# A Fourier mixing block in f32: the mix projection with its weights standing and the tokens moving, and two modulation vectors summed mostly on TensorE

## The chip, the cores and the metric

One core of a Trainium2 chip runs the whole kernel. The metric is the time of one execution on the device in microseconds (us); lower is better. Everything is f32 in memory. The large products are made of "f32r" parts: each operand is split into a high part and a low rest, and three one-pass products stand for one f32 product. The mix projection, the row sums and the transposes use plain f32 matmuls, which the trace shows as two records each (transposes as one).

## The reference, cut to what matters

512 tokens (N), 2048 channels (D), one layer of kind 0. The modulation vectors come from `c` by a 2048 x 12288 weight matrix, of which each vector takes 2048 columns.

```python
mod_x = silu(c) @ w_ada + b_ada
sh1, sc1, ga1, sh2, sc2, ga2 = split(mod_x, 6)
hx = rmsnorm(x, g_norm_mix) * (1 + sc1) + sh1
f  = fftn(hx.reshape(1, n, 4, 512), axes=(1, 3), norm='ortho').real
x  = x + ga1 * (f.reshape(1, n, 2048) @ fno_w_out)
h2 = rmsnorm(x, g_norm_ffn) * (1 + sc2) + sh2
x  = x + ga2 * (square(relu(h2 @ w_ffn_in)) @ w_ffn_out)
return rmsnorm(x, g_final)
```

## The kernel before, in words

Each engine has its own program, ordered by hand; semaphores join them. SP issues nearly all loads in one fixed order (`units`, with the mix tiles put between by `mix_after`). A load of 1 MiB goes into one of four slots (`raw`), and before load u SP waits until load u - 4 is consumed (`consumed`, line 369); whatever comes later in the list waits behind it. Mix tiles have four slots of their own (`load_mix`, line 395), freed by PE.

The stages, in order:

- To about 113 us: norm of x, the transform along the tokens, scale 1, the transform along the channels, and most of shift 1. The channel transform leaves cosine and sine parts for half of the tokens (`fe`, `fd`); the other half follows from symmetry, so that the projection has an even part and an odd part, whose sum and difference are the two token halves.
- Mix projection. 16 units (d, q): output columns 512d to 512d + 511, quarter q of the channels. A unit loads 1 MiB of `w_mix`; VectorE turns it into two combinations (`mix_sums`, lines 921 and 924). PE holds 128 tokens of `fe` or `fd` as weights and moves 512 columns of `w_mix`: four matmuls in `even_part` (line 1439), four in `odd_part` (1450) and two for a single middle row (`row_part`, 1460); with q = 3, three more for the first channel row. A bank holds 128 tokens x 512 channels, so the gate 1 vector has to be spread over all partitions (`row_sums`, line 1375). When a d is complete, ScalarE and VectorE combine, gate and add it to x (`combine`, `update_x`), and ScalarE squares it for the norm (line 577).
- Beside it the vectors gate 1, scale 2 and shift 2. A vector's load of 1 MiB is one weight row tile k (128 rows x 2048 columns; 8 KB to a partition), or two half rows of shift 2 (4 KB pieces); VectorE multiplies it by silu(c) and adds (`gemv`, line 823; `shift2_unit`, line 1020). The last five tiles of scale 2 go to PE (`gemv_rows`, line 1325): four matmuls with 32 equal weight columns, each in its own column group of the array, 512 columns moved by each.
- The turn to the FFN: last update, squares, root, `diag` (line 1072).
- First sweep (`up_step`, line 1561): 16 steps k. For each, PE turns 128 channels of x by matmuls with `diag` (`turn_tokens`, line 1534), ScalarE scales, shifts and makes the high part (lines 635 and 639), VectorE the low part (line 1085), and PE makes 12 products of 512 columns. The up weights are split by `up_high` and `up_low` (lines 607 and 1061). The second half of shift 2 is still added by VectorE in the sweep. At its end ScalarE takes the relu in two halves (line 656).
- The rest of the FFN: 15 periods of up and down products, then the final norm.

GpSimd writes x to HBM (line 462) for the end and loads the rows of gate 2 into `gate_w` (line 466).

## Time and profile before

| | |
|---|---|
| median of 3 runs | 1648.82 us (1647.47 to 1649.15) |
| span of the profiled execution | 1651.0 us; no other time of it is given |
| PE busy | 1606.8 us, 97% |
| VectorE busy | 1266.2 us, 77% |
| ScalarE busy | 545.4 us, 33% |
| moved by DMA | 272.64 MB, 165 GB/s over the span |

All times below count from the start of the span. "Busy" does not count waiting. Matmuls overlap each other in the trace, so what a matmul costs is read from one start to the next, not from its duration. `PEld` is the loading of weights, beside PE. A releaser ("<-") is what an idle engine waited for last.

### The profile page before, as it was taken

How to read it: one execution, taken by the hardware profiler on the slowest of the kernel's cores; microseconds unless marked ns; L12 is line 12 of the kernel's file. 1: busy time of each engine (PE TensorE's matmuls, PEld its weight loads, DVE VectorE, ACT ScalarE, POOL GpSimd, SP SyncE). 2: the span in 40 equal slices, each digit the busy share in tenths (PEclk: the TensorE clock that was granted, in tenths of full speed). 3: DMA queues.
4: the chain of work that ended last, by engine and by line, in shares of the span. 5: the costliest groups of instructions: out<-in, count | busy, mean ns of one | idle time of the engine just before them, and what ended most of it. 6: DMA issues, size and time to landing. Idle time of an engine off the chain costs nothing.

```text
span 1651.0 us, 18364 instructions
## 1 busy us (share of the span) xinstructions
PE 1606.8 (97%) x7009; PEld 1235.1 (75%) x7009; DVE 1266.2 (77%) x1168; ACT 545.4 (33%) x659; POOL 16.8 (1%) x30
## 2 busy tenths in 40 slices
PE   6989999999999999999999999999999999999997
PEld 5653332688888888888888888888888888888875
DVE  6758996748888888886868686868677777777878
ACT  5420002453333333333333333333333333333332
POOL 0000000100000000000000000000000000000000
PEclk9999999999999999999999999999999999999998
DMA  9999997924544444342323233323223323333352
GB/s 355 362 409 342 410 340 271 351 97 129 177 132 174 135 171 146 135 128 79 124 85 118 92 111 101 102 102 102 102 102 102 102 102 102 102 102 102 103 203 102
DMA packets 96970, 272.64 MB, mean 165 GB/s; under 512 B 4332, under 2 KB 5660, under 8 KB 85020
## 3 DMA queue, kind: packets, MB, share of 16 engines
q1 hardware_dynamic: 93664, 249.91, 42.3%
q0 software_dynamic: 3120, 22.07, 3.8%
q8 instruction: 30, 0.49, 0.1%
q14 instruction: 12, 0.10, 0.0%
q10 hardware_dynamic: 144, 0.07, 0.0%
HBM read 263.64 MB, written 8.39 MB: 165 GB/s over the span
## 4 chain that ended last, share of the span: by engine, by line
PE 87%; DVE 8%; DMA 3%; issue 2%; ACT 1%; SPq 0%; DVEq 0%; ACTq 0%
PE banks L1307 16%; PE banks L1308 16%; PE banks L1309 16%; PE banks L1613 11%; PE banks L1615 11%; PE banks L1617 11%; DMA raw<-in_w_ada 2%; DVE acc_s L823 1%; DVE acc_a L823 1%; DVE acc_b L1020 1%; PE banks L1534 1%; PE banks L1325 1%; DVE mixw L921 1%; DMA mixw<-in_w_mix 1%; PE banks L1450 1%
## 5 line engine op out<-in xcount | busy, mean ns | idle before, releaser
L1146 DVE TENSOR_TENSOR stp<-raw,stp 128x1024 fp32r<-128x1024 f32 x330 | 402.0, 1222 | 154.9 <-ACT stp L690 152.2
L690 ACT ACTIVATE stp<-raw 128x1024 fp32r<-128x1024 f32 x330 | 343.0, 1054 | 521.7 <-PE banks L1309 231.3
L1307 PE MATMUL banks<-acts,stp 128*128 128x512 f32 x1024 | 399.7, 390 | 0.0
L1308 PE MATMUL banks<-acts,stp 128*128 128x512 f32 x1024 | 398.4, 389 | 0.0
L1309 PE MATMUL banks<-acts,stp 128*128 128x512 f32 x1024 | 398.4, 389 | 0.0
L1613 PE MATMUL banks<-stp,hid 128*128 128x512 f32 x840 | 326.8, 389 | 0.0
L1615 PE MATMUL banks<-stp,hid 128*128 128x512 f32 x840 | 326.8, 389 | 0.0
L1617 PE MATMUL banks<-stp,hid 128*128 128x512 f32 x840 | 326.8, 389 | 0.0
L1167 DVE TENSOR_TENSOR dacc<-dacc,banks 128x1024 f32<-128x1024 f32 x202 | 245.5, 1215 | 14.2 <-PE banks L1617 14.2
L1309 PEld LDWEIGHTS banks<-acts,stp 128*128 128x128 f32 x1024 | 192.2, 188 | 40.0
L1307 PEld LDWEIGHTS banks<-acts,stp 128*128 128x128 f32 x1024 | 192.3, 188 | 39.8 <-DVE stp L1146 0.4
L1308 PEld LDWEIGHTS banks<-acts,stp 128*128 128x128 f32 x1024 | 192.2, 188 | 39.4
L1613 PEld LDWEIGHTS banks<-stp,hid 128*128 128x128 f32 x840 | 157.7, 188 | 32.9 <-DVE stp L1146 0.2
L1617 PEld LDWEIGHTS banks<-stp,hid 128*128 128x128 f32 x840 | 157.7, 188 | 32.7
L1615 PEld LDWEIGHTS banks<-stp,hid 128*128 128x128 f32 x840 | 157.7, 188 | 32.7
L668 ACT ACTIVATE hid<-hsum 128x512 fp32r<-128x512 f32 x45 | 28.5, 632 | 138.1 <-DVE hsum L1109 93.5
L823 DVE SCALAR_TENSOR_TENSOR acc_s<-raw,silu,acc_s 128x2048 f32<-128x2048 f32 x27 | 63.4, 2349 | 5.1 <-DMA raw<-in_w_ada 3.3
L1439 PE MATMUL banks<-mixw,fe 128*128 128x512 f32 x128 | 63.5, 619 | 1.8 <-DVE w_first L956 1.0
L1450 PE MATMUL banks<-mixw,fd 128*128 128x512 f32 x128 | 62.6, 614 | 0.0
L1122 DVE TENSOR_TENSOR raw<-raw 128x1024 f32<-128x1024 f32 x30 | 36.7, 1223 | 32.0 <-DMA raw<-in_w_ffn_out 32.0
L1097 DVE TENSOR_TENSOR sq<-sq 128x1024 f32<-128x1024 f32 x32 | 37.8, 1221 | 29.5 <-ACT sq L656 29.5
L668 ACT ACTIVATE hid<-sq 128x512 fp32r<-128x512 f32 x60 | 37.4, 624 | 68.5 <-DVE sq L1106 62.4
(190 smaller groups left out, 1227.1 us busy)
## 6 DMA issues: line engine op xcount, KB each, us to landing
raw<-in_w_ada SPq DMA_DIRECT2D x80, 1024.0 KB, 8.2
raw<-in_w_ffn_in SPq DMA_DIRECT2D x64, 1024.0 KB, 7.3
raw<-in_w_ffn_out SPq DMA_DIRECT2D x64, 1024.0 KB, 5.1
mixw<-in_w_mix SPq DMA_DIRECT2D x16, 1024.0 KB, 10.3
gate_w<-in_w_ada POOLq DMA_DIRECT2D x16, 1024.0 KB, 5.3
xres<-in_x SPq DMA_DIRECT2D x4, 1024.0 KB, 9.0
xmix_d<-xres POOLq DMA_DIRECT2D x4, 1024.0 KB, 12.7
xmix<-xmix_d SPq DMA_DIRECT2D x4, 1024.0 KB, 8.0
```

The costliest lines, as they stand in the source:

```text
L668: nc.scalar.activation(hid[:, a, :, 0, :], quarters[a], ACT.Copy).then_inc(h_hi, 1)
L690: nc.scalar.activation(stp[:, slot, 0, :, :], source.rearrange("p (a n) -> p a n", a=2), ACT.Copy).then_inc(w_hi, 1)
L823: ins = nc.vector.scalar_tensor_tensor(acc[:, :], source, silu[:, k:k + 1], acc[:, :], ALU.mult, ALU.add)
L1146: nc.vector.tensor_tensor(stp[:, slot, 1, :, :], source.rearrange("p (a n) -> p a n", a=2), stp[:, slot, 0, :, :].bitcast(F32), ALU.subtra ...
L1167: nc.vector.tensor_tensor(dst, dst, banks[:, b:b + 2, :], ALU.add).then_inc(d_read, 1)
L1307: nc.tensor.matmul(bank, w_hi_ap, m_hi, start=first, stop=False)
L1308: nc.tensor.matmul(bank, w_hi_ap, m_lo, start=False, stop=False)
L1309: return nc.tensor.matmul(bank, w_lo_ap, m_hi, start=False, stop=last)
L1450: mm = nc.tensor.matmul(banks[:, 4 * (d % 2) + 2 + tt, :], fd[:, 2 * q + i, tok], mixw[n % MIX_SLOTS][:, 2 + i, :], start=(q == 0 and i == 0),
L1613: nc.tensor.matmul(banks[:, b + tt, :], hid[:, q, kk, 0, tok], stp[:, slot, 0, kk, :], start=(kk == 0 and q not in (2, 3, 6)), stop=False, ...
L1615: nc.tensor.matmul(banks[:, b + tt, :], hid[:, q, kk, 0, tok], stp[:, slot, 1, kk, :], start=False, stop=False, skip_group_check=True)
L1617: mm = nc.tensor.matmul(banks[:, b + tt, :], hid[:, q, kk, 1, tok], stp[:, slot, 0, kk, :], start=False, stop=kk == HALF_T - 1, skip_group ...
```

## The change

The mix projection is turned around. Tile n (16 of them) is 128 output channels: PE holds 128 x 128 pieces of `w_mix` as weights and moves the frequencies: eight pieces and the first channel row over 257 columns (even part), eight over 255 (odd part), into one bank of 128 channels x 512 tokens. The host lays `w_mix` out so that a tile is 16 KB in a row for each partition, and gives a turned copy of x (`x_turned`, four loads of 1 MiB). Channels now lie on partitions: gate 1, scale 2 and shift 2 are single numbers of a partition. Gate 1 is summed by VectorE as before, then turned by PE. VectorE updates x (`xnew`), ScalarE squares it, VectorE adds the squares up, PE sums them over the partitions and spreads the inverse root (bank 4). PE turns each updated tile back (`turn_back`) to be written to HBM. Scale 2 and shift 2 come in eight blocks v of 512 columns (scale 2 for even v), each in four loads q of four row tiles (2 KB pieces): 32 loads, of which VectorE adds three ((0,0), (1,0), (2,0)) and PE 29; a load is 16 matmuls of 32 weight columns by 128 moved columns. Nine of PE's are in tiles 10 to 15, two between the mix and the sweep, 18 in the sweep. VectorE now scales in the sweep (`h2_scaled`) and ScalarE adds the shift. `turn_tokens`, `row_part`, `combine`, `update_pairs`, `shift2_unit` and the spread gate go. The cosine table is a third smaller.

Lines taken out in `up_step` stand with a minus; of the rest only what is new or kept around it is shown, and blank lines are left out.

```diff
+    BLOCKS = [(j, b) for b in range(DB) for j in (SCALE2, SHIFT2)]
+    ROWS_BY_DVE = [(0,)] * 3 + [()] * 5
+    rows_by_pe = lambda v: [q for q in range(UK) if q not in ROWS_BY_DVE[v]]
...
+    loads = [("raw", w) for w in units]
+    loads.insert(len(loads) - SHIFT_LAST, ("mix", 0))
+    loads.append(("mix", 1))
+    gates = [("ada", GATE1, k) for k in range(DT)]
+    blocks = [("block", v, q) for v in range(len(BLOCKS)) for q in range(UK)]
+    for n in range(2, 10):
+        loads += [("raw", w) for w in gates[2 * (n - 2):2 * (n - 1)]] + [("mix", n)]
+        if n >= 6:
+            loads.append(("turned", n - 6))
+    for n in range(10, MU):
+        loads += [("mix", n)] + [("raw", w) for w in blocks[2 * (n - 10):2 * (n - 9)]]
+    left = blocks[2 * (MU - 10):]
     up_units = [("up", q) for q in range(DT // UK)]
+    tail = up_units[0:2] + left[0:12] + up_units[2:3] + left[12:] + up_units[3:4]
+    loads += [("raw", w) for w in tail]
+    units = [w for kind, w in loads if kind == "raw"]
...
+    GATE1_AT = 8
+    UPDATED = {9: (0, 1), 10: (2, 3), 11: (4, 5, 6), 12: (7, 8, 9), 13: (10, 11), 14: (12, 13), 15: (14,)}
+    BLOCKS_AT = {10: [(0, 1)], 11: [(0, 2), (0, 3)], 12: [(1, 1)], 13: [(1, 2), (1, 3)], 14: [(2, 1)],
+                 15: [(2, 2), (2, 3)]}
+    BLOCK_BY_DVE_AT = {0: 10, 1: 12, 2: 14}
+    BLOCK_ROWS_AT = {0: 11, 1: 13, 2: 15}
+    TURN_BLOCK_AT = {0: 12, 1: 14}
+    BLOCK_TURNED_AT = {0: 12, 1: 14}
+    LATE_BLOCKS = {1: [(3, 2), (3, 3)], 2: [(4, 0), (4, 1)], 3: [(4, 2), (4, 3)], 4: [(5, 0), (5, 1)],
+                   5: [(5, 2), (5, 3)], 7: [(6, 0), (6, 1)], 8: [(6, 2), (6, 3)], 9: [(7, 0), (7, 1)],
+                   10: [(7, 2), (7, 3)]}
+    LATE_ROWS_AT = {3: 1, 4: 3, 5: 5, 6: 8, 7: 10}
+    LATE_TURN = {3: 3, 4: 5, 5: 6, 6: 10, 7: 11}
+    LATE_TURNED_AT = {2: 2, 3: 3, 4: 5, 5: 7, 6: 10, 7: 11}
+    UP_LATE_AT = {4: 5, 5: 6, 6: 10, 7: 12}
...
+            for kind, w in loads[1:]:
+                if kind == "mix":
+                    load_mix(w)
+                elif kind == "turned":
+                    load_turned(w)
+                else:
+                    u = position[w]
+                    if u >= RAW:
+                        sp.wait_ge(*consumed(units[u - RAW]))
+                    load(w, u % RAW)
...
+            def mix_copy(n):
+                act.wait_ge(w_used, n + 1)
+                nc.scalar.activation(xnew[:, n, :], banks[:, n % MIX_BANKS, :], ACT.Copy).then_inc(mix_out, 1)
+            def square(n):
+                act.wait_ge(updated, 2 * (n + 1))
+                if n >= 2:
+                    act.wait_ge(square_added, n - 2)
+                dst = square_sum if n == 0 else (square_even, square_odd)[n % 2]
+                nc.scalar.activation(dst[:, :], xnew[:, n, :], ACT.Square).then_inc(square_made, 1)
...
+            for n in range(MU):
+                turned_now = UPDATED.get(n - 1, ())
+                if n == MU - 1:
+                    up_high(0)
+                    up_high(1)
+                for u in turned_now[:1]:
+                    back_copy(u)
+                mix_copy(n)
+                for u in turned_now[1:]:
+                    back_copy(u)
+                for v in range(len(BLOCKS)):
+                    if BLOCK_ROWS_AT.get(v) == n:
+                        rows_of_block(v)
+                if n == GATE1_AT:
+                    rows_of(3)
+                for u in UPDATED.get(n, ()):
+                    square(u)
+            square(MU - 1)
+            back_copy(MU - 2)
             up_high(2)
             act.wait_ge(mean_done, 3)
             nc.scalar.activation(rms[:, 1, :], mean[:, 1, :], ACT.Sqrt).then_inc(rms_done, 1)
+            back_copy(MU - 1)
...
             for k in range(DT):
+                h2_high(k)
+                for m in range(4, UPS):
+                    if UP_LATE_AT[m] == k:
+                        up_high(m)
+                for v in range(len(BLOCKS)):
+                    if LATE_ROWS_AT.get(v) == k:
+                        rows_of_block(v)
...
+            def turned_block(v):
+                j, b = BLOCKS[v]
+                tiles = slice(GT * b, GT * (b + 1))
+                dve.wait_ge(rows_turned, 5 + v)
+                sums = banks[:, 7, P * (v % 4):P * (v % 4 + 1)].rearrange("p (a r) -> p a r", a=GT)[:, :, 0]
+                nc.vector.tensor_tensor(mods[:, j, tiles], sums, vec_t[:, j * DT + GT * b:j * DT + GT * (b + 1)],
+                                        ALU.add).then_inc(mod_step, 1)
+                if j == SCALE2:
+                    dve.wait_ge(mod_step, mods_after(v) - 1)
+                    nc.vector.scalar_tensor_tensor(mods[:, j, tiles], mods[:, j, tiles], 1.0,
+                                                   vec_t[:, 7 * DT + GT * b:7 * DT + GT * (b + 1)], ALU.add,
+                                                   ALU.mult).then_inc(mod_step, 1)
...
+            def update_x(n):
+                dve.wait_ge(mix_out, n + 1)
+                if n % GT == 0:
+                    dve.wait_ge(turned_in[n // GT], 16)
+                even, odd, new = xnew[:, n, 0:HALF], xnew[:, n, HALF:N], half_new[:, n % 2, :, :]
+                nc.vector.scalar_tensor_tensor(new, even.unsqueeze(1).to_broadcast([P, 2, HALF]),
+                                               mods[:, GATE1, n:n + 1],
+                                               xt[:, n, :].rearrange("p (a n) -> p a n", a=2),
+                                               ALU.mult, ALU.add).then_inc(update_half, 1)
+                dve.wait_ge(update_half, n + 1)
+                nc.vector.scalar_tensor_tensor(even, odd, gate_minus[:, n:n + 1], new[:, 0, :],
+                                               ALU.mult, ALU.add).then_inc(updated, 1)
+                nc.vector.scalar_tensor_tensor(odd, odd, mods[:, GATE1, n:n + 1], new[:, 1, :],
+                                               ALU.mult, ALU.add).then_inc(updated, 1)
+            def add_square(n):
...
+            def h2_scaled(k):
+                if k >= 2:
+                    dve.wait_ge(h2_hi, k - 1)
+                    dve.wait_ge(h2_lo, k - 1)
+                nc.vector.scalar_tensor_tensor(hmod[:, k % 2, :], xnew[:, k, :], mods[:, SCALE2, k:k + 1],
+                                               banks[:, 4, :], ALU.mult, ALU.mult).then_inc(hmod_done, 1)
+            def h2_low(k):
+                dve.wait_ge(h2_hi, k + 1)
+                nc.vector.scalar_tensor_tensor(acts[:, k, 1, :], hmod[:, k % 2, :], mods[:, SHIFT2, k:k + 1],
+                                               acts[:, k, 0, :].bitcast(F32), ALU.add, ALU.subtract).then_inc(h2_lo, 1)
+            mix_sums(0)
+            mix_sums(1)
+            shift_vector()
+            gemv(GATE1, 0)
+            shift_token()
+            mix_sums(2)
+            gates_left = list(range(1, DT))
+            for n in range(MU):
+                for u in UPDATED.get(n - 1, ()):
+                    add_square(u)
+                for _ in range(2):
+                    if gates_left:
+                        gemv(GATE1, gates_left.pop(0))
+                if n <= GATE1_AT:
+                    mix_sums(n + 3)
+                elif GATE1_AT + 1 < n < MU - 2:
+                    mix_sums(n + 2)
+                if n == GATE1_AT + 1:
+                    gate_vector()
+                for v in range(len(BLOCKS)):
+                    if BLOCK_BY_DVE_AT.get(v) == n:
+                        for q in ROWS_BY_DVE[v]:
+                            block_unit(v, q)
+                    if BLOCK_TURNED_AT.get(v) == n:
+                        turned_block(v)
+                for u in UPDATED.get(n, ()):
+                    update_x(u)
+            up_low(0)
+            up_low(1)
+            update_x(MU - 1)
+            up_low(2)
...
+            up_low(3)
+            dve.wait_ge(inv_spread, 1)
+            dve.wait_ge(mod_step, mods_after(1))
+            h2_scaled(0)
             for k in range(DT):
+                for v in range(len(BLOCKS)):
+                    if LATE_TURNED_AT.get(v) == k:
+                        turned_block(v)
+                if k + 1 < DT:
+                    if (k + 1) % GT == 0:
+                        dve.wait_ge(mod_step, mods_after(2 * ((k + 1) // GT) + 1))
+                    h2_scaled(k + 1)
+                h2_low(k)
+                for m in range(4, UPS):
+                    if UP_LATE_AT[m] == k:
+                        up_low(m)
...
+            def even_part(n, first):
+                bank = banks[:, n % MIX_BANKS, 0:EVEN]
+                for i in range(F_TILES):
+                    nc.tensor.matmul(bank, mixw[n % MIX_SLOTS][:, 0, i, :], freq[:, i, 0:EVEN],
+                                     start=(first and i == 0), stop=False, skip_group_check=True)
+                return nc.tensor.matmul(bank, w0[:, P * n:P * (n + 1)], f0[:, :], start=False, stop=True,
+                                        skip_group_check=True)
+            def odd_part(n, first):
...
+            def block_rows_sum(v, q):
+                u = position[("block", v, q)]
+                mine = rows_by_pe(v)
+                pe.wait_ge(raw_full[u % RAW], filled[u])
+                if q == mine[0]:
+                    pe.wait_ge(rows_out, 4 + v)
+                for i in range(UK):
+                    for a in range(4):
+                        mm = nc.tensor.matmul(banks[32 * a:32 * (a + 1), 6, P * (v % 4):P * (v % 4 + 1)],
+                                              silu32[:, UK * q + i, :],
+                                              raw[:, u % RAW, COLS * i + P * a:COLS * i + P * (a + 1)],
+                                              start=(q == mine[0] and i == 0),
+                                              stop=(q == mine[-1] and i == UK - 1 and not ROWS_BY_DVE[v]),
+                                              skip_group_check=True)
+                mm.then_inc(gemv_pe, 1)
...
+            def turn_block(v):
+                pe.wait_ge(rows_out, 5 + v)
+                pe.wait_ge(mod_step, mods_after(v - 1) - v % 2 if v else MODS_GATE - 1)
+                nc.tensor.transpose(banks[:, 7, P * (v % 4):P * (v % 4 + 1)], block_rows[:, v % 2, :], ident[:, :])\
+                    .then_inc(rows_turned, 1)
+            def turn_back(n):
+                pe.wait_ge(updated, 2 * (n + 1))
+                if n >= 2:
+                    pe.wait_ge(back_out, n - 1 if n < DT - 1 else n)
+                for t in range(TT):
+                    mm = nc.tensor.transpose(banks[:, back_bank(n), P * t:P * (t + 1)], xnew[:, n, P * t:P * (t + 1)],
+                                             ident[:, :])
+                mm.then_inc(back_turned, 1)
...
+            for n in range(MU):
+                turned_now = UPDATED.get(n - 1, ())
+                pe.wait_ge(w_lo, n + 1)
+                if n >= MIX_BANKS:
+                    pe.wait_ge(mix_out, n - MIX_BANKS + 1)
+                mm = even_part(n, n >= 2)
+                if n == GATE1_AT + 1:
+                    turn_rows(3, 7)
+                for u in turned_now[:1]:
+                    turn_back(u)
+                for v, q in BLOCKS_AT.get(n, ()):
+                    block_rows_sum(v, q)
+                for v in range(len(BLOCKS)):
+                    if TURN_BLOCK_AT.get(v) == n:
+                        turn_block(v)
+                if n >= 2:
+                    mm = odd_part(n, False)
+                mm.then_inc(w_used, 1)
+                for u in turned_now[1:]:
+                    turn_back(u)
                 if n == GATE1_AT:
                     pe.wait_ge(gemv_step, SCALE1_STEPS + SHIFT1_STEPS + DT)
+                    add_share(6, acc_s, True).then_inc(gate_sum, 1)
+            block_rows_sum(3, 0)
+            turn_back(MU - 2)
+            block_rows_sum(3, 1)
+            turn_block(2)
+            pe.wait_ge(square_added, MU - 3)
+            pe.wait_ge(square_made, MU)
+            for t in range(TT):
+                for i, squares in enumerate((square_sum, square_even, square_odd)):
+                    mm = nc.tensor.matmul(banks[:, 4, t:t + 1], squares[:, P * t:P * (t + 1)], ones[:, 0:1],
+                                          start=(i == 0), stop=(i == 2), skip_group_check=True)
+            mm.then_inc(ssq_ready, 1)
+            turn_back(MU - 1)
             pe.wait_ge(diag_ready, 1)
+            for t in range(TT):
+                mm = nc.tensor.matmul(banks[:, 4, P * t:P * (t + 1)], ones[:, :], diag[:, t, :],
+                                      start=True, stop=True, skip_group_check=True)
+            mm.then_inc(inv_spread, 1)
...
             def up_step(slot, m, first):
                 for kk in range(2):
                     k = 2 * m + kk
                     if first:
-                        if k == S_TILES - 1:
-                            shift2_sums(1)
-                        if k + LEAD < DT:
-                            turn_tokens(k + LEAD)
+                        for v, q in LATE_BLOCKS.get(k, ()):
+                            block_rows_sum(v, q)
+                        for v in range(len(BLOCKS)):
+                            if LATE_TURN.get(v) == k:
+                                turn_block(v)
                         pe.wait_ge(h2_lo, k + 1)
```

## Rows read from the trace of the kernel before

**Rows 1.** The page's head: span, and busy time of each engine.
```profile
span 1651.0 us, 18364 instructions
...
PE 1606.8 (97%) x7009; PEld 1235.1 (75%) x7009; DVE 1266.2 (77%) x1168; ACT 545.4 (33%) x659; POOL 16.8 (1%) x30
```

**Rows 2.** Windows: stretch, busy us and (instructions) by engine; clock, DMA share, GB/s.
```profile
150.00:200.00 50.00, 50.00 (x112) 17.76 (x111) 48.60 (x30) 2.90 (x2) 0.00 (x0) 1.00 1.02 403
...
250.00:297.00 47.00, 43.27 (x114) 13.48 (x116) 30.98 (x27) 10.60 (x23) 0.00 (x0) 0.93 0.67 252
...
310.00:330.00 20.00, 20.00 (x114) 17.43 (x113) 16.74 (x18) 8.12 (x11) 0.00 (x0) 1.00 1.02 408
```

**Rows 3.** Waits of SP, 108 to 366 us: total, times, longest.
```profile
SPq L386 <- DVE acc_b L1020: 69.2, 16, 18.9
```

**Rows 4.** Timeline of PE: start, us, line, tiles, instructions.
```profile
116.59 1.06 PE L1325 MATMUL banks<-raw,silu 128*32 128x512 f32 x8
...
131.62 1.98 PE L1439 MATMUL banks<-mixw,fe 128*128 128x512 f32 x4 [0.95 <-DVE w_first L956]
...
208.80 1.88 PE L1439 MATMUL banks<-mixw,fe 128*128 128x512 f32 x4
210.51 1.88 PE L1450 MATMUL banks<-mixw,fd 128*128 128x512 f32 x4
...
295.34 2.78 PE L1325 MATMUL banks<-raw,silu_late 128*32 128x512 f32 x24
...
298.91 1.95 PE L1544 MATMUL banks<-ones,acc_b 128*128 128x1 f32 x16
...
303.29 4.57 PE L1534 MATMUL banks<-diag,xres 128*128 128x128 f32 x24 [1.94 <-DVE diag L1072]
307.62 0.48 PE L1307 MATMUL banks<-acts,stp 128*128 128x512 f32 x1
...
310.45 1.05 PE L1534 MATMUL banks<-diag,xres 128*128 128x128 f32 x8
311.26 0.48 PE L1307 MATMUL banks<-acts,stp 128*128 128x512 f32 x1
...
314.08 1.05 PE L1534 MATMUL banks<-diag,xres 128*128 128x128 f32 x8
```

**Rows 5.** Timeline of ScalarE: the second relu of the first sweep.
```profile
365.02 1.03 ACT L656 ACTIVATE sq<-banks 128x1024 f32<-128x1024 f32 x1 [1.63 <-PE banks L1309]
```

**Rows 6.** Groups of VectorE: line, tiles, count, busy us, mean ns, idle before.
```profile
L823 DVE SCALAR_TENSOR_TENSOR acc_s<-raw,silu,acc_s 128x2048 f32<-128x2048 f32 x27 | 63.4, 2349 | 5.1 <-DMA raw<-in_w_ada 3.3
...
L921 DVE TENSOR_TENSOR mixw<-mixw 128x1024 f32<-128x1024 f32 x16 | 19.5, 1219 | 12.0 <-DMA mixw<-in_w_mix 12.0
L894 DVE SCALAR_TENSOR_TENSOR modp<-spec,mods,modp 128x512 fp32r<-128x512 f32 x16 | 10.9, 746 | 2.1 <-ACT modp L538 2.1
```

**Rows 7.** Windows, columns as in rows 2; first while only 2 KB loads run.
```profile
256.00:260.00 4.00, 4.00 (x10) 1.52 (x8) 0.00 (x0) 0.00 (x0) 0.00 (x0) 1.00 1.05 388
...
280.00:285.00 5.00, 4.00 (x11) 1.31 (x12) 1.70 (x2) 0.03 (x1) 0.00 (x0) 0.51 0.99 393
```

**Rows 8.** Row sums in column groups, a weight load's min/median/max ns, four transposes.
```profile
93.34 1.07 PE L1325 MATMUL banks<-raw,silu 128*32 128x512 f32 x8
94.33 0.38 PE L1307 MATMUL banks<-modp,cost 128*128 128x256 f32 x1
...
119.24 0.66 PE L1341 MATMUL banks<-ident,rows 128*128 128x128 f32 x4 [0.72 <-ACT rows L529]
...
L1325 PEld LDWEIGHTS banks<-raw,silu x112: 106/109/151, 34.2 to 116.6; 128*32 128x32 f32 x112
```

**Rows 9.** Timeline of VectorE: the start of the norm's last chain.
```profile
301.68 0.17 DVE L789 TENSOR_REDUCE ssq<-ssq_part 128x4 f32<-128x16 f32 x1 [0.62 <-ACT block_junk L577]
```

**Rows 10.** DMA issues on the page: KB each, median us to landing.
```profile
raw<-in_w_ada SPq DMA_DIRECT2D x80, 1024.0 KB, 8.2
...
gate_w<-in_w_ada POOLq DMA_DIRECT2D x16, 1024.0 KB, 5.3
```

634 lines of the change are left out of this document (207 added, 427 removed).

## The prediction, made before the changed kernel had run

> **What bounds the kernel now.** I read the page first: TensorE is busy for 97% of the span [rows 1]. That is an average, and the change lies in the first 365 us, so I cut that part into stretches [rows 2]. From 150 to 250 us three things are full at once: PE 50 of 50 us, VectorE 48.6 of 50 us, and the DMA engines, which move 403 GB/s. From 250 to 297 us loads fall to 252 GB/s: the queue SP mostly waits for VectorE to free a buffer [rows 3]. From 310 us PE alone is full. The moments come from PE's timeline [rows 4]: mix units proper start at 131.6, the last mix matmuls end at 295.3, the first FFN product starts at 307.6, and one k of the first FFN sweep takes 3.63 us (310.45 to 314.08). The sweep ends when ScalarE takes its second relu, at 365.02 [rows 5]; I call it 364.7. After that neither code nor order changes but for waits that are long met, so the sum is about this one moment. Before 113 us little changes (a cosine table a third smaller).
>
> **Mix matmuls.** Two 512-column f32 matmuls take 1.71 us (208.80 to 210.51 [rows 4]), or 1.67 ns a column. Before, a unit has 10 of them (8.55 us), and each fourth 3 more. After, a tile has nine of 257 columns (3.86 us) and eight of 255 (3.41): 7.27 us. No row has f32 at 257; f32 at 128 columns takes 0.81 us for four (310.45 to 311.26 [rows 4]), 1.58 ns a column, so the rule by columns holds from both sides. The odd parts of tiles 0 and 1 run before 131.6, in place of the six matmuls of unit 0 that ran there. PE would so be through tile 8 at 131.6 + 2 x 3.86 + 7 x 7.27 = 190.2.
>
> **Loads set tile 9.** The last shift-1 row was there by 116.6 [rows 4], and mix tile 1 follows at about 118. Up to tile 9 SP issues 27 loads of 1 MiB: 16 gate rows, 8 tiles, 3 of the turned x, which is new. At 403 GB/s one takes 2.60 us: 188.2, and some 3 us for slots that VectorE frees late (it has 7.15 us of work a tile: two rows of 2.35 and the two tile sums of 1.22 [rows 6]) make 191. Then VectorE has the sums of tile 9 (2.45) and gate row 15 (2.35): 195.8, and PE stands before the gate sum for 5.6 us. Before, 3.7 us of idle PE between 250 and 297 us (43.27 busy of 47 [rows 2]) brought the clock down: granted 0.51 in the five us after it [rows 7], 2.4 us lost, and I add 0.7 for the way back. Tile 9 ends at 195.8 + 1.0 (gate sum) + 7.3 + 0.6 (turned rows) + 3.1 = 207.8.
>
> **Scale and shift on PE.** A block load needs 16 matmuls of 32 weights by 128 columns. Before, four of 512 columns ran in four column groups at once: 0.99 us from start to start [rows 8]; the columns per group are the same. Lower bound 0.85; upper bound 3.2 us, if they go one after another at the 0.2 us of a 128-column f32 matmul. I take 0.9, and 0.2 for each entry: a 32-column weight load lasts 109 ns [rows 8], about as long as one of the two records of a 128-column matmul (0.81 us for eight), so it can hide behind it.
>
> **Tiles 10 to 15** on PE: 6 x 7.27 = 43.6; turning back 14 tiles at 0.55 (four transposes took 0.66 with their tail [rows 8]) 7.7; nine block loads 9.3; three partial sums and two turns 1.3: 61.9, so 269.7. VectorE beside it: 14 updates at 1.6 (one 512-column op of 0.75 [rows 6], two of 256, which no row shows: between the 0.17 of a tiny op [rows 9] and 0.75, taken 0.42), 13 square sums of 0.7, four tile sums, three block loads of 2.7: 50 of 62 us, in an order where PE waits for updates and SP for blocks. Of the x that is written out, three pieces also share the DMA. I add 4 us (0 to 10): 273.7. Before it was 295.3: 21.6 us gained.
>
> **The turn to the FFN** was 12.3 us. After: copy, update and square of tile 15 (3.3); the rest of block (3,1), whose slot PE frees only inside tile 15 (1.0); 24 records of square sums, at 1.95 us for 16 with their tail (at 298.91 [rows 4]) 2.7; mean, root and diagonal, 1.6 before (301.68 to 303.29 [rows 4, 9]); up-weights step 3 on VectorE beside the diagonal matmuls (1.3); two scaled tiles and a low part (2.4): 12.3, with 0.6 for hand-overs 12.9. The first product starts at 286.6. The 64 diagonal matmuls of the old sweep go (0.81 a k); the 12 products of a k took 2.82 us with the switch ahead of them (311.26 to 314.08 [rows 4]), and I take 2.73.
>
> **The sweep gets work and loads instead.** SP's load (3,3) waits until up-weights step 3 has freed its slot, at 284.2, and all else is queued behind that wait. From there 18 loads must land before PE can do the last block sum at k = 10; one spilled quarter of x and one gate_w row share the way: 20 in all. Rows of 2 KB moved at 388 GB/s [rows 7], 2.70 us; the mixed stretch gave 2.60; I take 2.65. A lone load landed in 5.3 us [rows 10], so 2.5 us are latency. 284.2 + 2.5 + 53.0 = 339.7. After it: the sum 1.0, k = 10 to 15 at 2.73 (16.4), and two waits that are new. At k = 3, 5, 10 and 11 PE turns a block row and wants the low part of the same k, but VectorE first waits for that very transpose, adds the bias, scales tile k + 1, and only then makes it: 0.4 for transpose and hand-over, 0.2 each for bias and gain, 0.8 and 0.75 for the two tiles, so 2.4 us at k = 10 and, without the gain, 2.1 at k = 11. With 0.3 for transposes: **361.9**. PE alone would give 286.6 + 43.7 + 18.0 (18 loads) + 9.2 (four waits) + 0.5 = 358.0, so both limits are near.
>
> The sum: 361.9 - 364.7 = -2.8 us. The profiled execution has a span of 1651.0 us, and the median of the three runs is 1648.8, 2.2 less; I take the difference off the median: **1646.0 us**. About 0.2% (3.3 us) is what a measurement of this kernel can tell from no change, so this is just inside it.
>
> **Rivals.** (a) The late stream is free. If mix tiles wait for nothing after tile 9 and loads stay ahead of PE, the sweep starts 4 us earlier and ends at 282.6 + 43.7 + 18.0 + 0.5 + 4.5 = 349.3: 1633. For it: 21 us are saved ahead, and 310 to 330 us moved 408 GB/s [rows 2]. Against it: the wait for step 3 and 20 loads. 0.25.
>
> (b) The ring starves, and it gets slower. SP may ask for a pair of blocks only when PE has consumed the pair two before; PE does that between products. If a pair's round trip is 8.2 us of landing [rows 10] plus 4.7 us of PE, four slots give one load each 3.2 us, so 16 loads take 8.8 us more: sweep end 370.7, 1655. It decides from 2.79 us a load. For it: SP's long waits for its consumers [rows 3]. Against: landing in a full queue is itself mostly queueing. 0.22.
> The Trainium skill ("DMA: Bandwidth & Descriptors", "Where 436 GB/s comes from") puts the HBM side at about 358 GB/s for a core; an estimate by that is 2.93 us a load and 5.6 us more than mine, also slower; this trace, with 388 and 403, does not agree.
>
> (c) The 128-column block matmuls run one after another: 3.2 us a load, 2.3 more on 18 loads, with the sweep then bound by PE: 358.0 + 41.4 = 399.4, and nine in the mix stage add 20: 1704. Against it: the 0.99 us for four. 0.05.
> The Trainium skill ("TensorE: Matmul & The Clock Gate", "Back-to-back issue gap") gives about 81 ns for each load-and-matmul pair at 128 columns; an estimate by that is 2.6 us for 32 records, near this rival. The four 512-column matmuls cannot show it.
>
> (d) My forecast's neighbourhood, 1641 to 1652: 0.48.
>
> **How the numbers follow.** Faster by over 0.2%: all of (a) and 0.16 of (d): 0.41. Slower: (b), (c) and 0.05 of (d): 0.32. Same: 0.27. The range takes in (a) and (b): 1632 to 1658, which leaves out (c) and tails.
>
> **What would show it.** In the changed profile: f32 mix matmuls of 257 columns at 0.43 us spacing; an idle PE before the gate sum at about 190 to 196 and a low clock behind it; last mix matmul near 274; first product near 287; block loads at 0.9 to 1.1 us on PE; SP's gap before (3,3), then about 390 GB/s to 340; PE idle at k = 3, 5, 10, 11 with VectorE as releaser; relu near 362. I am wrong if the last block load lands before 330, if a block load costs PE over 1.5 us, or if the mix stage ends before 268 or after 281.

## The result, and the profile after

The changed kernel takes 1661.14 us (median of 4, 1658.24 to 1663.93) where the kernel before takes 1648.99 (4 runs): ratio 1.007, 95% interval 1.0053 to 1.0087. It is slower by 12 us; 1646.0 was predicted, in a range of 1632 to 1658. The profiled execution took 1659.18 us with a span of 1657.3; time and span differ by 1.8 to 2.1 us in every run that follows. Below, "after" is the changed kernel. Ratios are of runs side by side and carry the intervals; a difference in us from after is one of medians from different batches, after's being of four runs, so one of 1 or 2 us says little.

The page's head, and windows as in [rows 2]:

```profile
span 1657.3 us, 20535 instructions
PE 1591.6 (96%) x8056; PEld 1304.4 (79%) x8056; DVE 1228.7 (74%) x1199; ACT 545.6 (33%) x661; POOL 17.6 (1%) x30
```
```profile
150.00:200.00 50.00, 45.18 (x205) 37.62 (x204) 36.70 (x22) 4.18 (x7) 0.00 (x0) 0.97 1.02 401
200.00:250.00 50.00, 45.08 (x395) 38.45 (x395) 37.09 (x59) 12.83 (x23) 1.37 (x2) 0.97 0.71 267
250.00:297.00 47.00, 38.24 (x328) 31.89 (x330) 27.33 (x44) 15.40 (x26) 4.67 (x6) 0.85 0.78 281
310.00:330.00 20.00, 16.31 (x196) 12.62 (x197) 8.09 (x13) 5.35 (x8) 0.00 (x0) 0.85 0.98 350
```

PE has 15 us less to do, so the change did remove work. But PE, VectorE and the DMA engines are no longer full together in any window: from 200 to 250 us all three have slack, and loads run at 267 GB/s. Something holds the loads back that is neither engine nor bandwidth.

PE's timeline, and ScalarE's second relu, which answer [rows 4, 5]:

```profile
194.62 1.93 PE L1353 MATMUL banks<-acc_s,ones 128*32 128x512 f32 x8 [4.82 <-DVE acc_s L840]
196.48 4.36 PE L1456 MATMUL banks<-freq,mixw 128*128 128x257 f32 x16
...
204.99 3.63 PE L1456 MATMUL banks<-freq,mixw 128*128 128x257 f32 x16
208.46 0.60 PE L1458 MATMUL banks<-f,w 128*128 128x257 f32 x2
208.89 0.60 PE L1506 MATMUL banks<-ident,xnew 128*128 128x128 f32 x4
209.42 1.08 PE L1478 MATMUL banks<-raw,silu 128*32 128x128 f32 x32
210.43 1.77 PE L1464 MATMUL banks<-freq,mixw 128*128 128x255 f32 x7
```
```profile
273.78 0.60 PE L1506 MATMUL banks<-ident,xnew 128*128 128x128 f32 x4
277.79 1.08 PE L1478 MATMUL banks<-raw,silu 128*32 128x128 f32 x32 [3.41 <-DMA raw<-in_w_ada]
278.80 0.66 PE L1506 MATMUL banks<-ident,xnew 128*128 128x128 f32 x4
280.50 1.08 PE L1478 MATMUL banks<-raw,silu 128*32 128x128 f32 x32 [1.04 <-DMA raw<-in_w_ada]
...
291.61 0.76 PE L1328 MATMUL banks<-acts,stp 128*128 128x512 f32 x1 [2.63 <-DVE acts L1058]
```
```profile
371.35 1.03 ACT L677 ACTIVATE sq<-banks 128x1024 f32<-128x1024 f32 x1 [1.63 <-PE banks L1330]
```

The marks against the forecast: tile 9 starts at 196.5 (195.8 + 1.0 forecast) and ends at 205.0 (207.8), the mix ends at 273.8 (273.7), the first product stands at 291.6 (286.6), the sweep ends at 371.35 (361.9 forecast; the kernel before 365.02 [rows 5]). The 6.3 us between the two relus are the whole difference of the spans, 1657.3 and 1651.0. So the mark at the end of the mix was hit, and 9.4 us came in after it. What PE waits for from 131 to 372 us, and SP likewise (us in total, times, longest), which answers [rows 3]:

```profile
PE banks L1328 <- DVE acts L1058: 9.6, 5, 2.6
PE banks L1478 <- DMA raw<-in_w_ada: 6.8, 4, 3.4
PE banks L1506 <- DVE xnew L1007: 6.1, 3, 3.6
PE banks L1353 <- DVE acc_s L840: 4.8, 1, 4.8
```
```profile
SPq L391 <- PE banks L1478: 57.5, 24, 7.2
SPq L391 <- DVE acc_b L1035: 53.6, 3, 20.1
SPq L391 <- DVE acc_s L840: 51.1, 14, 9.6
SPq L391 <- DVE stp L1042: 32.6, 4, 15.5
```

Three waits of SP take 53.6 us, 20.1 the longest. In the kernel before the same name stood at 69.2, but in 16 waits [rows 3]: 4.3 us each on average, with one of 18.9, where each of these three is long (15.9 at the least).

### The profile page after: what moved, and what is told of

Same layout as the page of the kernel before. It is cut to its first block, busy times and chain, and to the rows that moved or that the text cites. A ratio compares the mean times of both kernels' runs of the same rounds, so it can differ in the third digit from the quotient of the medians.

```text
span 1657.3 us, 20535 instructions
## 1 busy us (share of the span) xinstructions
PE 1591.6 (96%) x8056; PEld 1304.4 (79%) x8056; DVE 1228.7 (74%) x1199; ACT 545.6 (33%) x661; POOL 17.6 (1%) x30
## 4 chain that ended last, share of the span: by engine, by line
PE 89%; DMA 6%; DVE 4%; ACT 1%; issue 0%; SPq 0%; DVEq 0%
PE banks L1328 16%; PE banks L1329 16%; PE banks L1330 16%; PE banks L1627 11%; PE banks L1625 11%; PE banks L1629 11%; DMA mixw<-in_w_mix 3%; DMA raw<-in_w_ada 3%; PE banks L1456 2%; PE banks L1464 2%; PE banks L1478 1%; DMA xres<-in_x 0%; DVE acc_a L840 0%; DVE mixw L947 0%; PE banks L1458 0%
## 5 line engine op out<-in xcount | busy, mean ns | idle before, releaser
L1456 PE MATMUL banks<-freq,mixw 128*128 128x257 f32 x256 | 59.0, 384 | 1.0 <-DVE f L983 0.9
L1464 PE MATMUL banks<-freq,mixw 128*128 128x255 f32 x256 | 58.8, 383 | 0.9 <-DVE mixw L950 0.9
## 6 DMA issues: line engine op xcount, KB each, us to landing
mixw<-in_w_mix SPq DMA_DIRECT2D x16, 1024.0 KB, 12.9
xres<-in_x SPq DMA_DIRECT2D x4, 1024.0 KB, 10.4
```

What stands on the lines that cost most here:

```text
L1456: nc.tensor.matmul(bank, mixw[n % MIX_SLOTS][:, 0, i, :], freq[:, i, 0:EVEN], start=(first and i == 0), stop=False, skip_group_check=True)
L1464: mm = nc.tensor.matmul(banks[:, n % MIX_BANKS, EVEN:N], mixw[n % MIX_SLOTS][:, 1, i, :], freq[:, i, EVEN:N], start=(first and i == 0), st ...
```

## The experiments

The kernel before ran beside each batch on the same chip, with medians of 1649.9 to 1650.7 us. Ratios are to it; in brackets is the 95% interval. After itself stands at 1.007 [1.0053, 1.0087].

**First: VectorE's order in the sweep, and the turn.** The three waits with the plainest names are DVE's: acts, xnew, acc_s.

`e1_low_first`, the low part ahead of the turned block and the next scaling:

```diff
             for k in range(DT):
+                h2_low(k)
                 for v in range(len(BLOCKS)):
                     if LATE_TURNED_AT.get(v) == k:
                         turned_block(v)
...
                     h2_scaled(k + 1)
-                h2_low(k)
```

> The changed kernel, with one order turned: in the first FFN sweep VectorE makes the low part of step k before it takes up a turned block row and scales tile k + 1. Theory A (PE is the bound of the sweep and stands in the waits for VectorE that the block rows brought, 9.6 us in all in the changed kernel's profile): those waits all but vanish and the time falls by 5 to 9 us against the changed kernel (1661), to 1652 to 1656. Theory B (the late loads bound the sweep): the waits go, PE waits for DMA instead, and the time falls by less than 3 us, to 1658 or more.

Measured: 1655.78 us, 1.0032 [1.0014, 1.005]: 5.4 us less. Waits for acts fell from 9.6 to 6.4 us; those for raw rose from 6.8 to 8.2. That is at the upper edge of theory A's range (1652 to 1656).

`e2_up3_early`, up-weights step 3 ahead of the last updates:

```diff
-            back_copy(MU - 2)
             up_high(2)
+            up_high(3)
+            back_copy(MU - 2)
```

> The changed kernel, with step 3 of the up weights made by ScalarE and VectorE right behind step 2, ahead of the norm's root and not behind it, so that its raw slot is free some 7 us earlier and the late block loads (queued behind that slot on SP) start earlier. Theory B (late loads bound the sweep): the time falls by 3 to 7 us, to 1654 to 1658. Theory A (PE bounds it, by its own work and by waits for VectorE): within 2 us of the changed kernel's 1661; the first block sums of the sweep wait less for DMA, the end moves by little.

Measured: 1660.59, 1.0063 [1.0048, 1.0079]: nothing that can be told, as theory A has it. In its trace load (3,3) goes out at 279.6 us in place of 289.3, and the last block load only 5 us sooner (335.8 for 340.9): the loads from the one to the other then take 3.31 us each in place of 3.03. The long wait before (3,3) is not by itself what bounds the sweep.

`e3_turned_later`, the turned x loaded from tile 9 on, one piece a tile, in place of tiles 6 to 9:

```diff
-        if n >= 6:
-            loads.append(("turned", n - 6))
+        if n == 9:
+            loads.append(("turned", 0))
...
-        loads += [("mix", n)] + [("raw", w) for w in blocks[2 * (n - 10):2 * (n - 9)]]
+        loads += [("mix", n)] + [("turned", n - 9)] * (n < 13)
+        loads += [("raw", w) for w in blocks[2 * (n - 10):2 * (n - 9)]]
```

> The changed kernel, with the four loads of the turned x moved back in SP's list: behind mix tiles 9, 10, 11 and 12 and not behind 6, 7, 8 and 9. The prediction's account (27 loads set the start of tile 9): three loads fewer, 7.8 us, so PE's wait before the gate sum (4.8 us in the changed kernel) goes, the clock stays up there, and tile 9 starts 5 us earlier; the mix stage ends 2 to 6 us earlier and the time falls to 1655 to 1659. Rival: VectorE, not DMA, is behind (it has 7.15 us of work a tile), then the gate sum still comes at 192 or later and the time moves by less than 2 us.

Measured: 1659.65, 1.0045 [1.0028, 1.0062]. The 4.8 us before the gate sum are gone, PE's waits for xnew rose from 6.1 to 8.5, and the second relu came at 373.6. The median is just above the account's range (1655 to 1659) and 1.5 us below after: here the wait that ended early mostly handed its time to the next one.

`e4_quarter_loads`:

```diff
+                if w[0] == "block" and w[1] >= 3:
+                    src, dst = src[:, 0:1, :], dst[:, 0:1, :]
```

> The changed kernel, with each block load from v = 3 on bringing only the first of its four row tiles (256 KB for 1024 KB); PE's work stays, and it sums what lies in the slot, so scale 2 and shift 2 beyond the first three blocks are not the reference's. Theory B (late loads bound the sweep): the sweep shortens by over 8 us, the time falls to 1651 or below. Theory A (PE's own work and the waits for VectorE bound it): PE's 7 us of waits for block loads go, no more: 1653 to 1658.

Measured: 1652.43, 1.0007 [0.9991, 1.0022]: 8.7 us less. Waits for raw 0, those for acts still 9.4. That lies between the two theories (1651 or below, 1653 to 1658) and decides neither, but supply is worth more than any of VectorE's waits.

**Second: the clock.** Over the runs of one kernel the span follows the mean granted clock: after ran 1656.2 us at 0.987 and 1662.1 at 0.982, and before has a median clock of 0.993, after one of 0.986. Span times clock was 1637 us for before and 1635 for after, near the forecast's difference of 2.8. It looked like the answer, so I filled PE's idle stretches with work that nobody reads.

`e7_filled`, with 20 such products before the gate sum, 5, 15, 5 inside tiles 12 to 14, 14 and 4 before blocks (3,0) and (3,1), 10 before the first product and 5 or 7 at k = 3, 5, 10, 11:

```diff
+            def fill(bank, count):
+                for _ in range(count):
+                    nc.tensor.matmul(banks[:, bank, 0:P], ones[:, :], ident[:, :], start=True, stop=True,
+                                     skip_group_check=True)
```

> The kernel after with TensorE kept at work where it idled: products of ones with the identity matrix, 128 columns each, into PSUM banks that nobody reads, as many as the trace of after has idle time before the sum for gate 1 (4.8 us), behind three of the weight tiles, before the two blocks of units 3 (3.4 and 1.0 us), before the first product of the hidden layer (2.6 us) and before its steps 3, 5, 10 and 11. The outputs don't depend on them. Nothing that was waited for comes earlier: loads, VectorE's xnew and acts are as late as before. Theory C (what the sum of the prediction lacks is TensorE's granted clock, which falls after each new idle stretch and stays low while the work on the path goes on): the mean clock rises from 0.9855 to 0.991 or more, the window from 280 to 300 us from 0.66 to over 0.9, and the median falls from 1661 to between 1649 and 1655 us, ratio to before 1.000 to 1.004. Theory W (the new waits themselves are the loss, the clock only goes with them): the waits stay, the filling can only add to them, and the median stays at 1660 to 1664 us, ratio 1.007 to 1.009, whatever the clock shows.

Measured: 1658.39, 1.0038 [1.0022, 1.0053], clock 0.993. The clock came up as far as theory C wanted. The median fell by 2.7 us of the 6 to 12 and lies in neither theory's range; the ratio fell by 0.0032 (5.3 us) and is inside C's.

`e10_before_filled`, the same in the kernel before:

```diff
                     even_part(n, 0)
+                    fill(2, 14)
                     late_step(1)
...
+            fill(0, 8)
             pe.wait_ge(diag_ready, 1)
             turn_tokens(0)
```

> A control: the kernel before with its own two idle stretches of TensorE near the end of the mix filled in the same way (14 such products before the gemv that waits 3.7 us for its load, 8 before the turning of the tokens that waits 1.9 us for diag). The outputs don't depend on them. Theory C: the records of 281 to 290 us ran at half clock, some 4 us of work that took twice its time, so about 2 to 3 us come back: median 1646 to 1647.5, ratio 0.998 to 0.999, mean clock 0.995 or more. Theory W: 1649 to 1650, ratio 1.000. If this kernel gains as much as the filled form of after, the clock does not explain the difference between the two kernels.

Measured: 1647.29, 0.9981 [0.9969, 0.9993], clock 0.996: 3.4 us less than before. By medians the control gains as much as `e7_filled`, by ratios 0.0019 against 0.0032. With both kernels filled, the changed one still stands 0.0057 above the other (1.0038 less 0.9981), where unfilled it is 0.0070. So most of the difference is not the clock's; whether the rest is, these intervals leave open. Nor is span times clock a constant of the kernel: over the runs of `e7_filled` it is 1645 us, for after's 1635.

`e5_quarter_sums`:

```diff
+                late = v >= 4 or (v == 3 and q >= 2)
-                for i in range(UK):
+                for i in range(1 if late else UK):
```

> The kernel after, its late loads as they are, but of each of the 18 late loads TensorE sums only the first of its four row tiles; three quarters of the late block sums are left out of the output. It takes away the work of the sums and leaves their loads: 18 loads of 1.0 us at full clock on TensorE less three quarters, 13 us of TensorE's work. Theory S (the sweep is bound by TensorE's own work, as the prediction's sum had it): span shorter by 8 to 13 us, median 1648 to 1653. Theory L (the late loads arrive too late, the work between them fits into the waits): the waits for raw grow by what the sums lose, median 1656 to 1661, with idle time before the sums over 15 us in place of 6.8. Theory C adds that more idle time lowers the clock: below 0.985, which takes back part of any gain.

Measured: 1658.32, 1.0042 [1.0029, 1.0056]. 13 us of PE's work gone, 2.8 us gained; waits for raw rose from 6.8 to 10.0 us. Neither theory had it whole: the gain is L's, the waits did not reach the 15 and more that it asked for.

**Third: orders and filling together.** `e9_orders_filled` is e1, e2, e3 and the filling in one, with fewer products before the gate sum and in the sweep (what its expectation calls the high part of the last two xnew tiles is e2's order, up-weights step 3); `e8_orders` the three orders alone; `e12_best` adds 8 products in the wait for diag and has 5, not 10, before the first product; `e11_chain_filled` has only the filling from 274 to 291 us (14, 4, 8, 10), in after. `e13_quarter_best` is `e12_best` with the loads of `e4_quarter_loads`.

> The kernel after with its orders mended and the rest filled: h2_low before the turned block and the next scaling, the high part of the last two xnew tiles sooner, the turned loads later, and dummy products as in the filled kernel (4 in place of 20 before the sum for gate 1, 2 in place of 5 to 7 before each of steps 3, 5, 10, 11). The outputs don't depend on the dummy products. Theory C: span times clock was 1634.5 us for after and each of the three orders alone, so with the clock at 0.992 the span is 1634 / 0.992 = 1647 and the median 1647 to 1651 us, ratio 0.999 to 1.001. Theory W: the orders alone gave 1656 to 1660 us, the dummies add to that or do nothing: 1654 to 1660 us, ratio 1.003 to 1.006.

> The kernel after with its three orders mended and nothing filled: h2_low before the turned block and the next scaling, the high part of the last two xnew tiles sooner, the turned loads later. It parts what the mended and filled kernel gained (1650.6 us against 1661.1) into orders and filling. Theory A (the two add up: each order alone gave 5.4, 0.5 and 1.5 us, the filling alone 2.7): 1653 to 1655 us, ratio 1.0015 to 1.003. Theory C, in the form that is left (filling works only where the orders have left little idle time, so it gave less alone): 1657 or more, and then the clock below 0.987.

> The mended and filled kernel with 8 more dummy products in the wait for diag (there the clock still fell: 0.50 from 284 to 288 us) and 5 in place of 10 before the first product (at half clock the ten took 4.5 us, longer than the wait they filled). The outputs don't depend on them. If the clock holds through 283 to 290 us, first product at 287 and not 289.6: median 1647.5 to 1649 us, ratio to before 0.998 to 0.9995. If it falls all the same: 1650 to 1652.

> The kernel after with TensorE filled only between the end of the mix and the first product: 14 and 4 dummy products before the two blocks of units 3, 8 in the wait for diag, 10 before the first product. The outputs don't depend on them. If the clock of this stretch is what the filling gave back (records from 283 to 297 us ran at half clock in the trace of after, 3.1 us lost in the squares, diag and the turning, 2.6 us in the first twelve products), the median falls by 2.5 to 5 us, to 1656 to 1658.5. If the idle time elsewhere (before the sum for gate 1, between the turned tiles, before steps 3, 5, 10 and 11) sets it: 1660 to 1662. The first product stands at 287 to 289 us in the first case, at 291 to 292 in the second.

> The same kernel with only the first of four row tiles of each late block loaded (units 3 and later); TensorE sums what lies in the buffer, so the late shifts of the output are not the reference's. In the kernel after alone this gave 8.7 us (1661.1 to 1652.4), at a clock of 0.988. If that was the supply of the late blocks, what is left of it here goes: TensorE waits 4.0 us for raw in the mended kernel, so 1644 to 1646 us. If it was mostly the clock and the order of VectorE, which are mended here: within 1.5 us of the same kernel with whole loads.

Measured: e9 1650.59, 0.9999 [0.9988, 1.0011]; e8 1652.27, 1.001 [0.9998, 1.0021]; e12 1652.09, 1.0015 [1.0006, 1.0024]; e11 1661.91, 1.0075 [1.0058, 1.0092]; e13 1644.07, 0.9963 [0.995, 0.9976]. e9 came as theory C had it (1647 to 1651), but e8 shows that the orders alone do nearly all of it. The three orders give 8.9 us without filling, more than the 7.4 of their sum, and came out below both ranges set for e8. Filling the chain alone gives nothing, though its clock held only in part (0.83 from 280 to 290 us, 0.66 in after), and in `e12_best` the clock is full where it matters, and the time no better than that of the orders alone (1647.5 to 1649 was expected of a clock that holds):

```profile
250.00:297.00 47.00, 41.69 (x453) 36.75 (x452) 26.43 (x41) 16.11 (x28) 3.35 (x4) 1.00 0.84 304
297.00:372.00 75.00, 69.39 (x749) 54.98 (x748) 36.15 (x52) 22.95 (x32) 1.09 (x2) 1.00 0.81 294
```

What remains is supply: quarter loads give 8.0 us here as they gave 8.7 in after, and e13 is in the range that its expectation gave to supply. But the bandwidth is there (401 GB/s until 200 us, 267 after it), so the loads must be going out late.

**Fourth: why they go out late.** SP's timeline in after (start, duration, loads):

```profile
191.55 3.41 SPq L391 DMA_DIRECT2D raw<-in_w_ada  x2
195.00 3.38 SPq L409 DMA_DIRECT2D mixw<-in_w_mix  x1
215.98 1.25 SPq L391 DMA_DIRECT2D raw<-in_w_ada  x2
217.28 0.50 SPq L409 DMA_DIRECT2D mixw<-in_w_mix  x1
219.99 1.24 SPq L391 DMA_DIRECT2D raw<-in_w_ada  x2
221.27 1.07 SPq L409 DMA_DIRECT2D mixw<-in_w_mix  x1
242.45 0.92 SPq L391 DMA_DIRECT2D raw<-in_w_ada  x2
243.42 0.50 SPq L409 DMA_DIRECT2D mixw<-in_w_mix  x1
245.79 2.08 SPq L391 DMA_DIRECT2D raw<-in_w_ada  x2
263.84 0.92 SPq L391 DMA_DIRECT2D raw<-in_w_ffn_in  x2
```

and VectorE's, where the sums of the first units of blocks 0, 1 and 2 and the tile sums that wait for weights stand:

```profile
213.63 2.33 DVE L1035 SCALAR_TENSOR_TENSOR acc_b<-raw,silu,acc_b 128x512 f32<-128x512 f32 x3
...
226.21 1.23 DVE L947 TENSOR_TENSOR mixw<-mixw 128x1024 f32<-128x1024 f32 x1 [5.70 <-DMA mixw<-in_w_mix]
...
240.10 2.32 DVE L1035 SCALAR_TENSOR_TENSOR acc_b<-raw,silu,acc_b 128x512 f32<-128x512 f32 x3
...
253.94 1.23 DVE L947 TENSOR_TENSOR mixw<-mixw 128x1024 f32<-128x1024 f32 x1 [4.58 <-DMA mixw<-in_w_mix]
...
261.48 2.33 DVE L1035 SCALAR_TENSOR_TENSOR acc_b<-raw,silu,acc_b 128x512 f32<-128x512 f32 x3
```

SP issues nothing for 17.6, 20.1 and 15.9 us, and each time goes on as VectorE ends a block unit (215.9, 242.4, 263.8). The load due next takes the buffer that this unit holds, four loads on; VectorE sums it at tile 10, 12 or 14, though it could a tile sooner (in the next run it does, and never waits for its load). Behind that load stand the mix tiles, for which VectorE then waits (5.7 and 4.6 us), which puts its next block unit off again.

`e16_blocks_early`:

```diff
-    BLOCK_BY_DVE_AT = {0: 10, 1: 12, 2: 14}
+    BLOCK_BY_DVE_AT = {0: 9, 1: 11, 2: 13}
```

> The kernel after with one line changed: the first unit of blocks 0, 1 and 2, which VectorE sums, is summed at tiles 9, 11 and 13 of the mix in place of 10, 12 and 14; nothing is left out and nothing else moves. Theory Q (SyncE's queue): in the trace of after SyncE stood still from 198.4 to 216.0 and from 222.3 to 242.5 us for those sums, because the next block's load takes the buffer that they read, and every load behind it, weight tiles of the mix too, stood with it (267 GB/s from 200 to 250 us against 401 before that). Summed one tile sooner the two stalls lose about 7 and 11 us, the late blocks land by as much sooner, and the waits for raw (6.8 us) and for weight tiles go: median 1650 to 1656 us. Theory A (only VectorE's order in the sweep and TensorE's own work count, the loads would wait for their buffers later anyway): 1659 to 1662, with the 9.6 us of waits for acts unchanged.

Measured: 1648.5, 0.999 [0.998, 1.0]: **12.6 us less from one line**, more than theory Q's best. SP, PE and ScalarE in it, and then the waits of PE and of SP:

```profile
207.46 3.70 SPq L391 DMA_DIRECT2D raw<-in_w_ada  x2
211.20 0.50 SPq L409 DMA_DIRECT2D mixw<-in_w_mix  x1
220.21 1.24 SPq L391 DMA_DIRECT2D raw<-in_w_ada  x2
...
247.73 4.24 SPq L391 DMA_DIRECT2D raw<-in_w_ffn_in  x2
```
```profile
279.09 0.76 PE L1328 MATMUL banks<-acts,stp 128*128 128x512 f32 x1 [2.63 <-DVE acts L1058]
```
```profile
358.06 1.03 ACT L677 ACTIVATE sq<-banks 128x1024 f32<-128x1024 f32 x1 [1.63 <-PE banks L1330]
```
```profile
PE banks L1328 <- DVE acts L1058: 9.6, 5, 2.6
PE banks L1353 <- DVE acc_s L840: 4.8, 1, 4.8
PE banks L1478 <- DMA raw<-in_w_ada: 2.4, 2, 2.2
```
```profile
SPq L391 <- DVE acc_b L1035: 18.6, 3, 10.4
```

Of the 53.6 us of the three stalls 18.6 are left, 10.4 of them in the first; the first product is 12.5 us sooner and the sweep as long as it was (79.0 and 79.7 us). The waits for acts and acc_s are the same to a tenth: they were in the forecast, and rightly so.

`e19_block0_early` and `e20_block1_early` move one unit each, `{0: 9, 1: 12, 2: 14}` and `{0: 10, 1: 11, 2: 14}`:

> The kernel after with only block 0's first unit summed on VectorE a tile sooner (tile 9 in place of 10). In the trace of after its stall of SyncE lasted 17.6 us, in that of the kernel with all three moved the load behind it went out at 207.5 in place of 216.0. If each stall costs what it holds back: about 5 us of the 12.6, so 1654 to 1657.5 us. If only the longer second stall counts, because the mix of TensorE catches up after the first: 1659.5 or more. If the first is the one that pushes the second: 1650 or less.

> The kernel after with only block 1's first unit summed on VectorE a tile sooner (tile 11 in place of 12); its stall of SyncE was 20.1 us. If each stall costs what it holds back: about 7 of the 12.6 us, 1652.5 to 1656. If only the longer second one counts: 1648 to 1650. If the first is the one that matters: 1659 or more.

Measured: 1655.79, 1.0034 [1.002, 1.0049], and 1659.93, 1.0048 [1.0032, 1.0064]: 5.3 and 1.2 us. The first came as costed. The second came in the range where the first unit is the one that matters (1659 or more); what it gains by itself can't be told from nothing. The up-weights behind the third stall, here of e19 and then of e20, tell why:

```profile
257.85 0.92 SPq L391 DMA_DIRECT2D raw<-in_w_ffn_in  x2
```
```profile
262.86 0.92 SPq L391 DMA_DIRECT2D raw<-in_w_ffn_in  x2
```

They go out at 263.8, 262.9, 257.9 and 247.7 us in after, e20, e19 and e16, so 1.0, 6.0 and 16.1 us sooner, and the medians are 1.2, 5.3 and 12.6 us lower (the first products come 1.9, 6.7 and 12.5 us sooner). The order is clear; that the numbers match this well is more than the noise warrants. As far as these four traces go, a stall counts by what it leaves of the last one. Block 2's unit alone was not moved in a run, so its own share stays open; e20 leaves block 2 at tile 14, and most of the gain of its shorter second stall is lost there.

`e17_early_orders` is `e16_blocks_early` with the three orders, `e18_early_filled` that with sparing filling, `e15_quarter_both` is after with e4 and e5 together:

> The same line in the kernel with the three orders mended (1652.3 us). Theory Q: block loads of a quarter were worth 8.0 us there with filling (1652.1 to 1644.1), which is what a supply in time can give, so 1645 to 1649 us, ratio to before 0.995 to 0.999, and TensorE's waits for raw under 2 us. Theory A: 1651.5 to 1653.

> The kernel of the run before it, with TensorE filled sparingly (2, 6 and 2 dummy products behind tiles 12, 13 and 14, 4 before the sum for gate 1, 4 and 4 before the blocks of units 3, 8 in the wait for diag, 8 before the first product, none in the sweep; the outputs don't depend on them). In the earlier kernels filling gave 1.7 us (orders), 2.7 (after) and 3.4 (before) or nothing. Expected 1644 to 1648 us; if it adds nothing here either, the same as the run before it within 1 us.

> The kernel after with both a quarter of each late block load and a quarter of each late block sum; three quarters of both are left out of the output. Alone they gave 8.7 and 2.8 us. If supply and TensorE's work bound the sweep in turn (either alone is caught by the other), both together give more than their sum, 12 to 18 us: 1643 to 1649 us. If they are independent, 11.5 us: 1649.5. If VectorE's chain from scaling to low part (12.5 us of waits for acts at the least) takes over, under 10 us: 1651 or more.

Measured: **e17 1640.99, 0.9937 [0.9923, 0.995]**, which beats both kernels with nothing left out, by more than theory Q gave it (1645 to 1649); e18 1643.03, 0.9949 [0.9935, 0.9962], so filling adds nothing; e15 1642.65, 0.9947 [0.993, 0.9964]. In e17 theory Q's bound on the waits for raw failed: 4.9 us of them are left, not under 2. e15 gives 18.5 us where the parts give 8.7 and 2.8: in the sweep supply and PE's sums bound in turn, and one alone is caught by the other. The traces say the same: from the first product to the second relu after takes 79.7 us, e4 75.1, e5 78.2 and e15 65.7.

## Why the prediction was wrong, by its own steps

- **Mix matmuls**: right. 257 columns, 16 records in 3.47 us (204.99 to 208.46), 0.434 a matmul, forecast 0.43.
- **Loads set tile 9**: right, and with three loads fewer ahead of it (e3) the wait is gone. PE stands 4.8 us before the gate sum (forecast 5.6), which then runs at 1.2 GHz (granted clock 0.50 from 194.6 to 196.5 us): 1.86 us, against 0.97 at full clock for the eight such records at 297.94 in the kernel before. The low clock itself was put too high: behind the gate sum tile 9 took 8.5 us, where the sum has 11.0, of which 3.1 for the clock, so it ended 2.8 us ahead of the forecast.
- **Scale and shift on PE**: right. 32 records in 1.01 us (209.42 to 210.43), forecast 0.9 + 0.2 for each entry. Rival (c) is out. The Trainium skill ("TensorE: Matmul & The Clock Gate", "Back-to-back issue gap") has some 81 ns for a load-and-matmul pair at 128 columns, and an estimate by that is 2.6 us. With 32-column weights this trace shows 32 ns a pair.
- **Tiles 10 to 15**: the mark was hit (273.8 for 273.7), and that was luck: tile 9 ended 2.8 us early (205.0 for 207.8), and the six tiles took 68.8 us where the sum has 61.9 + 4. "I add 4 us (0 to 10)" stood for "an order where PE waits for updates and SP for blocks". **This is the step that failed**: the wait for a block was a small term of the mix alone, and SP's queue was not stepped through block by block, with the loads that stand behind each wait. In e16, where the stalls are short, the six tiles take 61.5 us (204.1 to 265.6) and the turn 13.5 in place of 17.8. So what e16 takes off the stalls is worth 7.3 us in the mix and 4.3 in the turn: 11.6, where the sum has 4 for all of the waits.
- **The turn**: 286.6 forecast, 291.6 measured, so 17.8 us for 12.9. The sum took blocks (3,0) and (3,1) as landed; PE waits 3.4 and 1.0 us for them, because their loads go out behind the third stall. Some of the rest is low clock: the square sums took 3.7 us, against 2.6 in e16.
- **The sweep**: 75.3 us forecast, 79.7 measured. Load (3,3) goes out at 289.3 (284.2), the last at 340.9. From the one to the other 17 steps take 51.6 us, 3.03 a load. The 2.65 of the sum, taken from bandwidth, is the second term that failed, and e16 does not mend it (50.7 us for the same 17 steps, sweep 79.0). With a quarter of the bytes (e4) a load still takes 2.70 us, with a quarter of PE's sums (e5) 2.79, with both (e15) 2.29: neither bytes nor PE's sums alone set the pace. 3.03 is past the 2.79 us from which rival (b) decides, and near its 3.2, so its 0.22 was too low. That its sweep end, 370.7, is within 0.7 us of the trace is partly luck, since it has (3,3) going out 5 us sooner. And (b) named the ring in the sweep, while e16's 12.6 us came from the ring ahead of it.
- **The four waits of VectorE**: 9.2 us forecast in all; 9.6 measured with that before the first product, 7.0 without it.
- **The median**: the span rose by 6.3 us, the median by 12.2. The profiled execution of before was 2 to 4 us above what it usually takes (span 1651.0, where the median of its own batch is a span of about 1647 and that of the later ones 1648 to 1649), that of after 2 below. So 9.1 of the 15.1 us are the terms above (1657.3 against 1651.0 - 2.8), and 6 the choice of executions. The -2.8 itself should have been -3.1: the sum took the relu of [rows 5] as 364.7, and the row has 365.02.
- **The signs of being wrong** that it set itself (last block load landed before 330, a block load over 1.5 us, the mix ending before 268 or after 281) all stayed away, and it was wrong: none of them looked at what SP waited for.
- The Trainium skill ("DMA: Bandwidth & Descriptors", "Where 436 GB/s comes from") puts the HBM side at some 358 GB/s for a core, half of what two cores share. That is not what limits this core, which runs alone: after moves 401 GB/s from 150 to 200 us.

## What to carry to other kernels

When a queue's waits for one engine become few and long, step through that queue load by load: which buffer does the next load take, who holds it, at which place of that engine's program is it let go, and what stands behind it. A wait that PE never shows can be the one that sets the end, because it is paid later, as a late load in another stage. And a quantity that follows the time from run to run (here the clock) is not for that reason the cause of a difference between kernels: with both kernels filled, most of the difference stood. Last, a mark that is hit can hide two misses: compare how long each stretch took, and not only when it ended.

## What the runs showed of the hardware, unexpected

- The span of one and the same kernel follows its mean granted clock: 1656.2 us at 0.987, 1657.3 at 0.988, 1661.1 at 0.984 and 1662.1 at 0.982 in after. Raising the clock by filling need not bring the time with it: `e11_chain_filled` has a median clock of 0.990 and 1661.91 us.
- Keeping PE busy in the two idle stretches of the kernel before held the clock at 2.4 GHz through 280 to 290 us (it was 0.66 there) and gave 0.19% (0.9981 [0.9969, 0.9993]); in after and its variants the same gave from 2.7 us (by medians, `e7_filled`) down to nothing (e11, e12, e18), and at 1.2 GHz the filling itself ran long (ten products in 4.5 us in `e9_orders_filled`).
- A matmul of 32-column weights by 128 columns in one of four column groups costs 32 ns a record, with its weight load beside it.
